# A mixture-of-experts layer on one core: expert blocks of 32 rows on four column groups instead of 64 rows on two

## The reference

```python
tok = h.reshape(288, 1024)                      # h = x1 * (1 + s2) + b2
logits = tok @ w_router + b_router              # 32 experts
top_val, top_idx = top_k(logits, 4); gate = softmax(top_val)
for each expert e, for the rows x routed to it:
    hid = x @ w_e_in[e] + b_e_in[e]             # (1024 -> 2048), float32
    glu, lin = split(hid); glu = min(glu, 7); lin = clip(lin, -7, 7)
    act = glu * sigmoid(1.702 * glu) * (lin + 1)
    out = act @ w_e_out[e] + b_e_out[e]         # (1024 -> 1024)
y = sum over the 4 experts of a token: gate * out
x = layer_norm(alpha * x1 + g2 * y)
```

## Time and profile before

| | |
|---|---|
| median of 3 runs | 1511.62 us (1511.14 to 1512.0) |
| span of the profiled execution (first to last instruction) | 1511.2 us, 20451 instructions |
| PE busy / weight loads | 1319.9 us (87%) / 521.6 us (35%) |
| DVE / ACT / POOL busy | 478.5 (32%) / 218.0 (14%) / 48.0 us (3%) |
| read from HBM | 451.51 MB, 301 GB/s over the span |
| mean granted clock of PE | 0.935 |

### The profile page before, as it was taken

One profiled execution on the slowest core, in us unless ns is written; L12 is line 12 of the kernel. 1 busy time (PEld: TensorE's weight loads), 2 busy tenths in 40 slices (PEclk: granted clock), 3 DMA queues, 4 the chain that ended last, 5 costly groups with the idle time before them and its releaser, 6 DMA issues.

```text
span 1511.2 us, 20451 instructions
## 1 busy us (share of the span) xinstructions
PE 1319.9 (87%) x7748; PEld 521.6 (35%) x7749; DVE 478.5 (32%) x1186; ACT 218.0 (14%) x446; POOL 48.0 (3%) x80
## 2 busy tenths in 40 slices
PE   1698886935999999999999999999999999999992
PEld 0276333322333333333333333333333333333330
DVE  1355332463323323322322223222322232232236
ACT  0011121031111110111111101021111111111210
POOL 3500000030000000000000000000000000000000
PEclk9799895956999999999999999999999999999996
DMA  6940497037999499999999999967999997735050
GB/s 211 324 160 12 178 291 291 14 129 279 410 409 409 184 410 410 409 410 410 409 409 410 410 410 409 410 278 307 409 409 410 409 410 309 292 140 235 0 187 31
DMA packets 134083, 455.01 MB, mean 301 GB/s; under 512 B 18050, under 2 KB 24059, under 8 KB 133999
## 3 DMA queue, kind: packets, MB, share of 16 engines
q1 hardware_dynamic: 123376, 447.54, 75.9%
q10 hardware_dynamic: 10687, 7.22, 1.8%
HBM read 451.51 MB, written 3.79 MB: 301 GB/s over the span
## 4 chain that ended last, share of the span: by engine, by line
PE 57%; DMA 30%; DVE 5%; ACTq 2%; issue 2%; ACT 1%; SPq 1%; POOL 0%; DVEq 0%; POOLq 0%
DMA w<-in_w_e_out 29%; PE bank L1382 19%; PE bank L1345 16%; PE bank L1125 4%; PE bank L1304 3%; PE bank L1073 3%; PE bank L1257 2%; PE bank L1325 1%; PE bank L1173 1%; PE bank L1176 1%; PE bank L1110 1%; PE bank L1334 1%; PE bank L1367 1%; DMA w_odd<-in_w_ada 1%; SPq L337 1%
## 5 line engine op out<-in xcount | busy, mean ns | idle before, releaser
L1382 PE MATMUL bank<-w,mt 128*64 128x512 f32 x1216 | 283.1, 620 | 36.1 <-DMA w<-in_w_e_out 36.1
L1345 PE MATMUL bank<-w_even,mt 128*64 128x512 f32 x1344 | 296.4, 593 | 7.8 <-ACT mt L653 7.8
L1345 PE MATMUL bank<-w_odd,mt 128*64 128x512 f32 x1088 | 239.2, 592 | 0.0
L992 DVE TENSOR_SCALAR mt<-bank 128x512 f32<-128x512 f32 x38 | 26.3, 692 | 593.8 <-PE bank L1345 593.8
L1382 PEld LDWEIGHTS bank<-w,mt 128*64 128x64 f32 x1216 | 88.3, 143 | 208.7 <-issue 166.4
L1345 PEld LDWEIGHTS bank<-w_even,mt 128*64 128x64 f32 x1344 | 94.9, 137 | 182.4 <-issue 180.7
L959 DVE TENSOR_TENSOR xy<-bank,xy 128x512 f32<-128x512 f32 (+1 forms) x234 | 146.1, 678 | 8.8 <-PE bank L1304 8.8
L1304 PE MATMUL bank<-mt,gpickT 64*128 64x512 f32 (+1 forms) x468 | 129.6, 631 | 0.7 <-ACT mt L667 0.7
L1345 PEld LDWEIGHTS bank<-w_odd,mt 128*64 128x64 f32 x1088 | 76.2, 137 | 140.2 <-issue 137.7
L1325 PE MATMUL bank<-pick,hb 128*128 128x64 bf16 x1824 | 70.1, 194 | 14.1 <-DVE gpick L987 14.1
L1325 PEld LDWEIGHTS bank<-pick,hb 128*128 128x128 bf16 x1824 | 65.6, 99 | 44.2 <-issue 30.0
(11 more groups left out here) (247 smaller groups left out, 873.7 us busy)
## 6 DMA issues: line engine op xcount, KB each, us to landing
w_even<-in_w_e_in SPq DMA_DIRECT2D x64, 2048.0 KB, 17.6
w<-in_w_e_out SPq DMA_DIRECT2D x64, 2048.0 KB, 18.3
w_odd<-in_w_e_in SPq DMA_DIRECT2D x64, 2048.0 KB, 18.7
w_odd<-in_w_ada SPq DMA_DIRECT2D x12, 2048.0 KB, 7.8
w_even<-in_w_in SPq DMA_DIRECT2D x2, 2048.0 KB, 17.7
w_even<-in_w_in SPq DMA_DIRECT2D x8, 256.0 KB, 5.1
w_even<-in_w_in SPq DMA_DIRECT2D x2, 1024.0 KB, 8.8
w<-in_w_out SPq DMA_DIRECT2D x4, 512.0 KB, 14.6
```

The lines of the kernel that those rows point to most:

```text
L992: v.tensor_scalar(glu, bank[1][:, :], LIMIT, None, ALU.min).then_inc(m["glu"], 1)
L1345: ins = mm(bank[bk][64 * h:64 * h + 64, :], xT[:, SLOTS * k:SLOTS * (k + 1)], w1t[:, k, first + 512 * h:first + 512 * (h + 1)], start=Fals ...
L1382: ins = mm(bank[4][64 * h:64 * h + 64, :], aT[:, P * j + SLOTS * (k // 4):P * j + SLOTS * (k // 4) + SLOTS], w2t[:, k, 512 * h:512 * (h + ...
```

## The change

Blocks have 32 slots instead of 64 (`SLOTS = 32`), so an expert with c rows has ceil(c / 32) blocks, up to nine. The block count is worked out by one comparison with nine steps and a sum. All products of a block use four groups (NQ = 4) of the array, each with 32 stationary columns and a quarter of the output columns:

- the gather has `pick` (128 x 32, float32) as the stationary operand and h2 in float32 as the moving one, three token tiles x four groups of 256 columns. The rows come out with slots on partitions; they are copied, transposed by two 128-column transposes (`turn_x`) and copied again. The bf16 split with its ACT and POOL work is gone, and h2 has a buffer of its own;
- the up product does glu and lin in one: four groups of 2 x 256 columns in one bank, eight steps; the down product four groups of 256 columns;
- glu, lin, prod, act are 128 x 256; only two transposes of act are left;
- the combine has 32 stationary rows per group: each of four row groups writes a 128 x 256 piece to a bank of its own, for two token tiles, and the sample tile goes to a quarter of a bank per group, where it stays packed (32 rows x 4) until four copies at the end unpack it;
- PE's order in a block is up product, combine of the block before, transposes of gpick, of act, *gather of the next block*, down product with `turn_x` in its middle.

SyncE's order is the same with m["Ulo"] (first four contraction steps done) and m["U"] in place of m["G"] and m["L"]: `load_w1` now splits w1 by contraction steps instead of columns, two DMAs of 2 MiB per half with runs of 8 KB. Expert 1's w1 waits for the transposes of h2 instead of the split. The clearing of XY, outb and gpickT moves from DVE to POOL.

```diff
-SLOTS = 64
+SLOTS = 32
+NQ = 4
+DQ = D // NQ
+NBLK = 9
...
-                c = slice(D * half, D * (half + 1))
                 for j in range(2):
-                    sp.dma_start(w1v[par][:, 4 * j:4 * j + 4, c], src[:, 4 * j:4 * j + 4, c]).then_inc((ld_glu, ld_lin)[half][par], 16)
+                    r = slice(4 * half + 2 * j, 4 * half + 2 * j + 2)
+                    sp.dma_start(w1v[par][:, r, :], src[:, r, :]).then_inc((ld_lo, ld_hi)[half][par], 16)
...
-                sp.wait_ge(m["G"], v)
+                sp.wait_ge(m["Ulo"], v)
                 load_w1(0, 2 * i + 2, 0)
-                sp.wait_ge(m["L"], v)
+                sp.wait_ge(m["U"], v)
                 load_w1(0, 2 * i + 2, 1)
...
+            pool.wait_ge(lg_done, 3)
+            g.memset(outb, 0.0).then_inc(moe_zero, 1)
+            g.memset(gpickT[:, :], 0.0).then_inc(moe_zero, 1)
+            pool.wait_ge(ld["x1s"], 48)
+            g.memset(XY[:, :, :], 0.0).then_inc(y_zero, 1)
...
+            eng.wait_ge(m["gath"], 2)
+            a.activation(xg, bank[1][:, 0:DQ], ACT.Copy).then_inc(m["xg"], 1)
+            eng.wait_ge(m["xt"], 2)
+            a.activation(xT, bank[1][:, DQ:2 * DQ], ACT.Copy).then_inc(m["xT"], 1)
...
                     eng.wait_ge(m["glu"], n2)
                     eng.wait_ge(m["act"], n1)
                     a.activation(gsig, glu, ACT.Sigmoid, scale=SW_ALPHA).then_inc(m["sig"], 1)
                     eng.wait_ge(m["gT"], n2)
+                    a.activation(gpickT[:, :], bank[2][:, 0:NTOK], ACT.Copy).then_inc(m["gT_copied"], 1)
+                    eng.wait_ge(m["at"], n2)
+                    a.activation(aT, bank[3][:, 0:DQ], ACT.Copy).then_inc(m["aT"], 1)
+                    eng.wait_ge(m["gath"], n3)
+                    a.activation(xg, bank[1][:, 0:DQ], ACT.Copy).then_inc(m["xg"], 1)
+                    eng.wait_ge(m["xt"], n3)
+                    a.activation(xT, bank[1][:, DQ:2 * DQ], ACT.Copy).then_inc(m["xT"], 1)
                     eng.wait_ge(m["S2"], n2)
+                    a.activation(outb, bank[2][:, 0:DQ], ACT.Copy).then_inc(m["out"], 1)
...
+                    dve.wait_ge(m["gath"], n1)
+                    for t in range(3):
+                        v.tensor_scalar(pick[:, t, :], iota[:, bass.ds(at, SLOTS)], rkc[:, t, :], None, ALU.is_equal)
                     dve.wait_ge(m["gT"], n1)
...
                     ins.then_inc(m["pick"], 1)
+                    dve.wait_ge(m["comb"], n1)
+                    dve.wait_ge(m["aT"], n1)
+                    dve.wait_ge(m["y"], n1)
+                    add_y(m["y"])
+                    dve.wait_ge(m["U"], n2)
+                    dve.wait_ge(m["prod"], n1)
+                    v.tensor_scalar(glu, bank[0][:, 0:DQ], LIMIT, None, ALU.min).then_inc(m["glu"], 1)
+                    v.tensor_scalar(lin, bank[0][:, DQ:2 * DQ], LIMIT, -LIMIT, ALU.min, ALU.max).then_inc(m["lin"], 1)
...
+            def gather():
+                for t in range(3):
+                    for q in range(NQ):
+                        ins = mm(xps[SLOTS * q:SLOTS * (q + 1), 0:DQ], pick[:, t, :], h2[:, t, DQ * q:DQ * (q + 1)],
+                                 start=(t == 0), stop=(t == 2))
+                ins.then_inc(m["gath"], 1)
+            def turn_x():
+                for c in range(2):
+                    ins = nc.tensor.transpose(xps[:, DQ + P * c:DQ + P * (c + 1)], xg[:, P * c:P * (c + 1)], ident[:, :])
+                ins.then_inc(m["xt"], 1)
+            def combine():
+                for t in range(2):
+                    for q in range(NQ):
+                        mm(quads[:, q, DQ * t:DQ * (t + 1)], gpickT[SLOTS * q:SLOTS * (q + 1), T0[t]:T0[t] + P],
+                           outb[SLOTS * q:SLOTS * (q + 1), :], start=True, stop=True)
+                for q in range(NQ):
+                    ins = mm(aps[SLOTS * q:SLOTS * (q + 1), DQ:2 * DQ], gpickT[SLOTS * q:SLOTS * (q + 1), SEQ:NTOK],
+                             outb[SLOTS * q:SLOTS * (q + 1), :], start=True, stop=True)
+                return ins
...
+                    pe.wait_ge(sel_ready, e1)
+                    pe.wait_ge(m["lin"], n1)
...
+                    pe.wait_ge(m["xT"], n2)
+                    pe.wait_ge(ld_lo[p], w1)
                     for k in range(DK):
+                        if k == DK // 2:
+                            pe.wait_ge(ld_hi[p], w1)
+                        for q in range(NQ):
+                            ins = mm(hid[SLOTS * q:SLOTS * (q + 1), :], xT[:, P * (k % 2) + SLOTS * (k // 2):P * (k % 2) + SLOTS * (k // 2) + SLOTS],
+                                     w1t[:, k, :, DQ * q:DQ * (q + 1)], start=False, stop=(k == DK - 1))
+                        if k == DK // 2 - 1:
+                            ins.then_inc(m["Ulo"], 1)
+                    ins.then_inc(m["U"], 1)
                     pe.wait_ge(m["out"], n1)
                     pe.wait_ge(m["gT_copied"], n1)
+                    pe.wait_ge(m["y"], n2)
+                    combine().then_inc(m["comb"], 1)
+                    pe.wait_ge(m["pick"], n2)
...
+                    pe.wait_ge(m["act"], n2)
...
+                    pe.wait_ge(m["pick"], n3)
+                    gather()
+                    pe.wait_ge(m["gT_copied"], n2)
...
+                    pe.wait_ge(m["aT"], n2)
+                    pe.wait_ge(ld_w2, w2)
+                    for k in range(DK):
+                        if k == DK // 2:
+                            pe.wait_ge(m["xg"], n3)
+                            turn_x()
+                        for q in range(NQ):
+                            ins = mm(ops[SLOTS * q:SLOTS * (q + 1), 0:DQ], aT[:, P * (k % 2) + SLOTS * (k // 2):P * (k % 2) + SLOTS * (k // 2) + SLOTS],
+                                     w2v[:, k, DQ * q:DQ * (q + 1)], start=False, stop=(k == DK - 1))
                     ins.then_inc(m["S2"], 1)
```

More of the change, by code:

```diff
@@ L91, in hybrid_streaming_encoder_step @@
         vb_c = MT[:, 3840:3968]
-        xT, glu, gsig, sg, act, aT, outb, lin = (MT[:, 512 * j:512 * (j + 1)] for j in range(8))
-        hb = HB[:, 0:3072].bitcast(BF16).rearrange("p (t j d) -> p t j d", t=2, j=3)
-        hb_s = HB[:, 3072:3584].bitcast(BF16)
+        xg, xT, glu, lin, gsig, prod, act, aT, outb = (MT[:, DQ * j:DQ * (j + 1)] for j in range(9))
+        h2 = HB[:, 0:3072].rearrange("p (t d) -> p t d", t=3)
         prob = HB[:, 0:1024].rearrange("p (s h k) -> p s h k", s=2, h=2)
@@ L222, in hybrid_streaming_encoder_step @@
         m = {n: sem(f"m_{n}") for n in (
-            "cur", "pick", "gath_a", "gath_b", "xT_a", "xT_b", "G", "glu", "sig", "gs", "c01", "y01", "L", "lin_a", "lin",
-            "act_a", "act", "c2", "y2", "gT", "gT_copied", "T_a", "T_b", "aT_a", "aT_b", "S2", "out")}
+            "pick", "gath", "xg", "xt", "xT", "Ulo", "U", "glu", "lin", "sig", "prod", "act", "comb", "y", "gT", "gT_copied",
+            "at", "aT", "S2", "out")}
         sel_ready, cur_ready, top_done, gexp_done = (sem(n) for n in ("sel_ready", "cur_ready", "top_done", "gexp_done"))
@@ L1014, in _ @@
+                    v.scalar_tensor_tensor(out=prod, in0=lin, scalar=1.0, in1=glu, op0=ALU.add, op1=ALU.mult)\
+                     .then_inc(m["prod"], 1)
+                    dve.wait_ge(m["prod"], n2)
+                    dve.wait_ge(m["sig"], n2)
+                    dve.wait_ge(m["at"], n1)
+                    v.tensor_tensor(act, prod, gsig, ALU.mult).then_inc(m["act"], 1)
             with dve.Fori(0, NE // 2) as i:
@@ L1296, in _ @@
             pe.wait_ge(b3_done, 1)
-            for name in ("gath_a", "gath_b", "G", "c01", "L", "c2", "gT", "T_a", "T_b", "S2"):
+            for name in ("gath", "xt", "Ulo", "U", "gT", "at", "S2"):
                 pe.sem_inc(m[name], 1)
-            tiles = ((0, (3, 4)), (1, (5, 0)), (2, (6, 7)))
-            def combine(t, banks):
-                for h in range(2):
-                    ins = mm(bank[banks[h]][0:TS[t], :], gpickT[64 * h:64 * h + 64, T0[t]:T0[t] + TS[t]], outb[64 * h:64 * h + 64, :],
-                             start=True, stop=True)
+            hid, xps, ops, aps = bank[0], bank[1], bank[2], bank[3]
+            def gather():
[9 more added lines that the diff above has]
+            def combine():
+                for t in range(2):
+                    for q in range(NQ):
[4 more added lines that the diff above has]
+                             outb[SLOTS * q:SLOTS * (q + 1), :], start=True, stop=True)
                 return ins
@@ L1315, in moe @@
                     n2 = pe.snap(n + 2)
-                    pe.wait_ge(m["y01"], n1)
-                    pe.wait_ge(m["pick"], n2)
-                    for k in range(DK):
-                        if k == 4:
-                            pe.wait_ge(m["lin"], n1)
-                        out = bank[0 if k < 4 else 2][:, SLOTS * (k % 4):SLOTS * (k % 4 + 1)]
-                        for t in range(2):
-                            for j in range(3):
```

(12 more changed lines are left out.)

230 lines of the change are left out of this document (69 added, 161 removed).

## The result

The changed kernel took 1604.69 us (median of 4 runs, 1600.73 to 1608.75), the kernel before 1511.38 (1510.74 to 1512.0): 1.0618 times as long, 95% interval 1.06 to 1.0636. The forecast was 1591, range 1550 to 1655.

The account below looks back on a forecast made before the run. The weight stream, stopped at experts of several blocks, was taken as the bound: expert 30's down product at 1470.1 us, its blocks and expert 31 to 1557.4, 33.5 for the tail and 0.4 more gave 1591 us, range 1550 to 1655.

Parts of the forecast that it names:

- start to T(1): From the kernel's start through expert 0 to the start of expert 1's first down product: 407.8 us.
- T(1) to T(30): From expert 1's first down product to expert 30's: 29 experts at 30.1 us plus stops of 189.4 us.
- T(30) to the last product's end: From expert 30's first down product: its five blocks 69.9 us, w2(31) 13.5, last down product 3.9.
- tail: After the last down product: outb copy, combine, add_y, sample-row copies and 26.7 us from L1033 on, 33.5 us in all.
- around the span: Difference between the profiled execution's span and the median run: 0.4 us.
- Rival 2: Loads of the next experts flow during extra blocks, which cost the stream nothing: about 1402 us, chance 0.03.
- Rivals 1: Up and down products: four column groups do not run at once (13.7 and 6.9 us): 1783 us, chance 0.04.
- 1b: Up and down products: a round of four takes a third longer than one product: 1645 us, chance 0.09.
- 4: Combine: its row groups are serial, 2.5 us a block: 1615 us; chance within the forecast's 0.83.
- Rival 3: Weight stream: it does not gain from 8 KB rows: 1610 us; chance within the forecast's 0.83.
- Rival 5: First down products: TensorE's clock stays up while it waits for w2: 1572 us; chance within the forecast's 0.83.
- the further block: Each additional block of the same expert: up product, chain to the next down product, down product, 16.1 us.

Follow-up runs that it names:

- e1: Changed kernel with every expert cut to its first block of 32 rows: 1319.1 us.
- e6: Kernel before with every expert held to its first block of 64 rows: 1363.1 us.
- e9: Changed kernel with no table load in the loop, gather waiting for pick alone, and w2 waited for in halves: 1553.9 us.
- e10: Changed kernel with no table load in the loop, gather waiting for pick alone, and w2 loaded and waited for in quarters: 1539.2 us.
- e7: Changed kernel with no table load in the loop and the gather waiting for pick alone, not gpick: 1584.3 us.
- e5: Kernel before with w1 loaded in 8 KB runs instead of 4 and the up product reordered to suit: 1499.4 us.
- e3: Changed kernel with one sigmoid ahead of the loop, so no activation table is loaded in it: 1586.2 us.
- e8: Kernel before with w1 in 8 KB runs and no table load in the loop: 1498.9 us.
- e12: Kernel before with w1 in 8 KB runs, no table load in the loop, w2 in quarters and w1 freed in quarters: 1477.8 us.

## Why the prediction was right, and where its terms were off

| term of the sum | forecast | profiled |
|---|---|---|
| start to T(1) | 407.8 | 405.0 |
| T(1) to T(30) | 1062.3 | 1065.5 |
| T(30) to the last product's end | 87.3 | 95.1 |
| tail | 33.5 | 33.3 |
| around the span | 0.4 | 1.9 |

- *The mechanism held.* The stream stands still from w2's landing to the last block's half up product, and e1 and e6 put the whole loss on further blocks. Rival 2 (further blocks hidden) is out: no byte moves at 496 to 524. Splitting the wait that the mechanism names (e9, e10) took 30 and 45 us off e7.
- *Up, down, combine.* 7.05, 4.1 with turn_x at full clock, 1.7, against 7.1, 3.9 and 2.0. Rivals 1, 1b and 4 are out: four column groups and four row groups run together. The Trainium skill (TensorE: Matmul & The Clock Gate, "Measured speedup vs the span model") has 3.07 for four row tiles and 2.38 for three column tiles; here the fourth group came nearly free, and the measurement decides.
- *Stream.* 30.12 us per one-block expert, forecast 30.1. Rival 3 is out, and e5 shows it without the rest of the change.
- *Start.* cum_ready at 337.6 (339) and the first up product at 348.0 (353): the gather ran at full clock, and the copies and transpose took less than the 4 + 2 us given to them. Of these 5 us only 2.8 arrive at T(1): expert 0's blocks took 2.2 longer than priced.
- *Stops.* Ten of them were to cost 189.4 us and cost 192. That is nearer than their parts, and in so far luck: the six two-block experts came out at 10.7 to 13.0 each (12.5), 3.8 less in all, the four three-block experts at 26.7 to 31.7 (28.6), 6.4 more. The first down product was priced at one value, 5.5. Where TensorE had waited 3 us or more for w2 it took 5.7 to 6.4, its first half mostly at half clock; where it had waited less than 2 us, 4.2. Rival 5 is out (granted clock 0.50 at 496), but for those short waits the clock did stay up.
- *The mis-sized term is the further block*, put at 16.1: 17.0 twice in expert 30, 18.5 there and 18.7 at expert 4, where the gather runs at half clock as well. The table load (1.1 us by e3) was not seen: the kernel before has 42 of them, but around the copies of the gathered rows, where e8 shows them to cost nothing. Without it the block takes 15.9, so the chain was near right but for the load that it put at nothing. And the last block of an expert gathers for the *next* one, whose ranks and picks DVE prepares later. Most of these gathers wait 3.5 to 4.0 us and then run mostly at half clock (up to 2.8 us). In a one-block expert w2 has still to land then, and this costs nothing; at expert 30 it stands on the path,

```profile
1541.10 2.78 PE L1284 MATMUL bank<-hb,pick 128*32 128x256 f32 x24 [3.57 <-DVE gpick L968]
```

and the block takes 20.8 from its up product to the end of its down product. That is past the 19 us which the prediction named as a sign of being wrong; the blocks before it are inside. The third term is made of these: blocks of 18.5, 17.0, 17.0 and 20.8 instead of four of 16.1 (+8.9), a warm first product (4.2 for 5.5, -1.3), and 0.1 in the last two pieces. The stream is idle there for some 79 us, not 70.
- *Around the span* 1.9 us, not 0.4. The 0.4 compared the span of one execution with the time of another; where both are on record for the same execution of the kernel before, they are 1.7 to 1.8 apart. The runs of after scatter over 8 us, so the median lies 4 above the profiled run. Nothing here explains that scatter, and table loads don't: without them e3 scatters over 1, but e9 over 11 and e10 over 8.

## What to carry to other kernels

Smaller tiles that fill the array better don't help where a stream is the floor; count instead how often they make the stream wait, and price each stop by what lies between the last byte's landing and the first buffer's release. That stretch is shortened cheaply by splitting waits, so that work runs while the rest lands and buffers come free piece by piece: with no engine faster, this took 45 us from the changed kernel (e7 to e10) and 21 from the other (e8 to e12). And take a gain apart before it is rebuilt around: of this change, the load in 8 KB runs was tried alone in the kernel before, and brought 12 us there. The earlier start and the shorter last blocks, 17 and 11 us with one block per expert, were not tried alone.

## What was not expected of the hardware

- The granted clock fell to 0.50 inside dense work, after pauses of 0.68 and 1.05 us with 0.44 us of transposes between; the gather then took 2.71 us instead of 1.50 (512.77, and 2.79 at 1486.06). With the same two pauses (0.69 and 1.04) at 1502 to 1505 it stayed at full clock and the gather took 1.50. So whether a short pause costs is not settled by its length alone. The Trainium skill (TensorE: Matmul & The Clock Gate, "Seeing it yourself") warns that clock events in traces can be unreliable; here the duration agrees with the granted clock.
- A table load came back in the loop for 30 of 51 blocks though the loop needs one set of functions only; one activation of that set ahead of it removed them all.
- 418 to 420 GB/s were held over 40 us from HBM into one core. The Trainium skill (DMA: Bandwidth & Descriptors, "Where 436 GB/s comes from") has the HBM side bind such transfers near 358, and in the same passage puts its own measurement of 425 for 16 MB near the fabric's rate of 435. The measurement here decides, and it is near the second.
